# Spreading the decay rows of two mixers with a selector of 128 partitions instead of 64

## What is computed

```python
gc = jnp.cumsum(g, axis=-1)
decay = jnp.exp(jnp.where(incl, gc[..., :, None] - gc[..., None, :], -jnp.inf))
```

```python
acum = jnp.cumsum(da, axis=2)
seg = jnp.exp(jnp.where(incl, acum[:, :, :, None] - acum[:, :, None, :], -jnp.inf))
```

## Time and profile before

| what | before |
|---|---|
| median of 3 runs | 2264.95 us (2264.87 to 2265.81) |
| profiled execution, its own time | 2268.4 us |
| span of the profiled execution | 2266.6 us |
| TensorE busy | 2178.9 us, 96% of the span |
| TensorE weight loads busy | 1984.3 us, 88% |
| VectorE / ScalarE / GpSimd busy | 65% / 59% / 47% |
| mean granted TensorE clock | 0.981 |
| DMA | 151 GB/s read over the span |

### The profile page before, as it was taken

How to read it: one execution, slowest core, us unless ns; L and a number is a source line. 1 busy time by engine, 2 the same in 40 slices (tenths; PEclk the granted TensorE clock), 3 DMA queues, 4 the chain that set the end, 5 groups by cost and what they waited for, 6 DMA issues and landing times.

```text
span 2266.6 us, 46015 instructions
## 1 busy us (share of the span) xinstructions
PE 2178.9 (96%) x14384; PEld 1984.3 (88%) x14384; DVE 1476.7 (65%) x3206; ACT 1342.9 (59%) x2734; POOL 1069.7 (47%) x827
## 2 busy tenths in 40 slices
PE   7989699999999999999899988999999999999998
PEld 6979599999999988888797767999999999888886
DVE  5756319985666577777765452199756665777776
ACT  6754355577777544444475664555687785444444
POOL 6841378987666600000065337799976665000000
PEclk9989899999999999999999999999999999999999
DMA  5510254555444566666544224555554445666664
GB/s 167 167 58 1 66 176 149 168 165 157 139 139 139 171 190 192 194 194 194 177 133 136 65 66 150 166 159 168 167 155 139 139 139 167 194 193 192 191 194 147
DMA packets 93872, 343.66 MB, mean 152 GB/s; under 512 B 10688, under 2 KB 10752, under 8 KB 93152
## 3 DMA queue, kind: packets, MB, share of 16 engines
q1 hardware_dynamic: 92592, 338.21, 48.5%
q0 software_dynamic: 912, 4.07, 0.6%
q10 hardware_dynamic: 288, 0.34, 0.0%
HBM read 341.53 MB, written 1.05 MB: 151 GB/s over the span
## 4 chain that ended last, share of the span: by engine, by line
PE 82%; POOL 7%; issue 5%; DVE 3%; ACT 2%; DMA 1%; POOLq 0%; DVEq 0%; ACTq 0%
PE bank L359 80%; POOL w_lo L1738 7%; PE bank L524 0%; PE bank L379 0%; DMA small<-in_ssd_d 0%; ACT w_hi L1368 0%; ACT arena L1394 0%; DVE arena L874 0%; ACT arena L1368 0%; DVE arena L989 0%; DVE arena L1190 0%; DVE arena L1029 0%; DVE arena L925 0%; DMA ring<-in_norm_final 0%; ACT arena L1528 0%
## 5 line engine op out<-in xcount | busy, mean ns | idle before, releaser
L1738 POOL TENSOR_TENSOR w_lo<-ring,w_hi 128x512 fp32r<-128x512 f32 x744 | 993.5, 1350 | 685.6 <-ACT w_hi L1368 673.9
L1368 ACT ACTIVATE w_hi<-ring 128x512 fp32r<-128x512 f32 x1280 | 804.4, 630 | 544.5 <-PE bank L359 542.7
L359 PE MATMUL bank<-hT_hi,w_hi 128*128 128x256 f32 x2688 | 780.0, 290 | 9.1 <-POOL w_lo L1738 7.0
L359 PE MATMUL bank<-hT_lo,w_hi 128*128 128x256 f32 x2688 | 761.3, 283 | 0.0
L359 PE MATMUL bank<-hT_hi,w_lo 128*128 128x256 f32 x2688 | 761.2, 283 | 0.0
L359 PEld LDWEIGHTS bank<-hT_hi,w_hi 128*128 128x128 f32 x2688 | 516.2, 192 | 20.1 <-POOL w_lo L1738 19.6
L900 DVE TENSOR_TENSOR w_lo<-ring,w_hi 128x512 fp32r<-128x512 f32 x536 | 374.9, 699 | 220.9 <-ACT w_hi L1368 213.9
L359 PEld LDWEIGHTS bank<-hT_lo,w_hi 128*128 128x128 f32 x2688 | 516.5, 192 | 0.0
L359 PEld LDWEIGHTS bank<-hT_hi,w_lo 128*128 128x128 f32 x2688 | 515.8, 192 | 0.0
L359 PE MATMUL bank<-w_hi,p_ag_hi 128*128 128x512 f32 x1024 | 398.4, 389 | 0.0
L359 PE MATMUL bank<-w_lo,p_ag_hi 128*128 128x512 f32 x1024 | 398.4, 389 | 0.0
(11 more groups left out here) (241 smaller groups left out, 2256.8 us busy)
## 6 DMA issues: line engine op xcount, KB each, us to landing
ring<-in_peer_u SPq DMA_DIRECT2D x256, 512.0 KB, 3.5
ring<-in_peer_v SPq DMA_DIRECT2D x256, 512.0 KB, 3.7
ring<-in_peer_wq SPq DMA_DIRECT2D x32, 512.0 KB, 3.5
ring<-in_gdn_qkv SPq DMA_DIRECT2D x24, 512.0 KB, 3.6
ring<-in_ssd_xbc SPq DMA_DIRECT2D x24, 512.0 KB, 3.6
ring<-in_ssd_z SPq DMA_DIRECT2D x16, 512.0 KB, 3.5
ring<-in_ssd_out SPq DMA_DIRECT2D x16, 512.0 KB, 3.6
ring<-in_gdn_z SPq DMA_DIRECT2D x8, 512.0 KB, 3.5
```

The source lines that it names most:

```text
L359: return pe.matmul(o, w, r, start=first, stop=last)
L1368: return act.activation(o, i, ACT.Copy, scale=scale)
L1738: pool.tensor_tensor(w_part[1][:, s, :], ring[:, n % RING, hf * 512:(hf + 1) * 512], w_part[0][:, s, :].bitcast(F32), ALU.subtract).then_i ...
```

## The change

`pick` gets 128 partitions, of which the lower 64 are zero, and `s_row` is all 128 partitions of `p_ag[0]`. So the matmul with `pick` has weights of 128 x 128 instead of 64 x 128, in both mixers. The products of the lower 64 partitions are zero times what lies in `p_ag[0]` there. ScalarE makes one more copy in each mixer, from a zero block of the identity (partitions 64 to 127, columns 0 to 31), and the waits for `picks` count 3 and 6 instead of 2 and 4. The zeroing in GDN covers 128 partitions instead of 64. Nothing changes places.

```diff
-        pick = sb("pick", [2 * SH, SH], F32R)[:, :]
-        s_row = flat(p_ag[0][0:2 * SH, :, :], "s t")
+        pick = sb("pick", [P, SH], F32R)[:, :]
+        s_row = flat(p_ag[0][:, :, :], "s t")
...
-                mm(bank[:, :], pick[:, h:h + 1].to_broadcast([2 * SH, P]), s_row[:, :], True, False)
+                mm(bank[:, :], pick[:, h:h + 1].to_broadcast([P, P]), s_row[:, :], True, False)
...
-                pe.wait_ge(picks, 2)
+                pe.wait_ge(picks, 3)
...
-                pe.wait_ge(picks, 4)
+                pe.wait_ge(picks, 6)
...
-                        mm(o, pick[:, h:h + 1].to_broadcast([2 * SH, P]), s_row[:, st * P:(st + 3) * P], True, False)
+                        mm(o, pick[:, h:h + 1].to_broadcast([P, P]), s_row[:, st * P:(st + 3) * P], True, False)
...
-                        dve.tensor_scalar(p_ag[0][0:2 * SH, 1, :], flat(const[0:2 * SH, 0:2, :], "m i"), 0.0, None, ALU.mult)
+                        dve.tensor_scalar(p_ag[0][:, 1, :], flat(const[:, 0:2, :], "m i"), 0.0, None, ALU.mult)
...
                 copy(pick[SH:2 * SH, :], const[SH:2 * SH, C_EYE, SH:2 * SH]).then_inc(picks, 1)
+                copy(pick[2 * SH:P, :], const[2 * SH:P, C_EYE, 0:SH]).then_inc(picks, 1)
```

## The result

| what | before | after |
|---|---|---|
| median of 4 runs each | 2265.38 us (2264.87 to 2266.22) | 2239.09 us (2238.46 to 2239.70) |
| profiled execution, its own time | 2268.4 us | 2239.61 us |
| span of the profiled execution | 2266.6 us | 2237.8 us |
| TensorE busy | 2178.9 us | 2149.9 us |
| mean granted TensorE clock | 0.981 | 0.982 |

The ratio is 0.9879, with a 95% interval from 0.9863 to 0.9894: 26.3 us faster between the medians. The forecast was 2238.2 us in a range from 2232 to 2249, so time, range and sign are right. The steps behind the number are less right than the number, as the experiments show.

The account below looks back on a forecast made before the run. TensorE's distances between matmul starts were taken to bound all SSD heads and GDN until head 4. SSD 24.9 plus GDN 1.85 gave 26.75 us off 2268.4, then 3.45 down to the runs' median: 2238.2 us, range 2232 to 2249.

Parts of the forecast that it names:

- What bounds the kernel: TensorE is the chain through all 32 SSD heads, 127.14 us, and the first five GDN heads, 20.73 us.
- The cause: Weight loads of 64 partitions can't run ahead among those of 128; the form alone makes the loader wait, 15.1 us in SSD.
- The broadcast rival: Loads of a broadcast column can't run ahead either; 16.0 us won in SSD, some 1.4 in GDN: 2248 us; chance 0.08.
- no effect: The form is not the cause, every distance between matmuls stays, time 2265 us; chance 0.06.
- A matmul with `pick`, SSD, 25.3 us: SSD heads: distances between matmul starts fall from 1.71 to 0.92 us, 0.79 us a head, 25.3 us for 32.
- the three bursts: SSD: ScalarE's table loads, as at head 10, leave its exponentials just in time; cost 0, upper bound 0.3 us each.
- a sign that it is wrong: TensorE waiting for ScalarE's exponentials at heads 13, 21 and 29, or `pick` still having 0.3 us or more before it.
- The last head: SSD head 31: TensorE is 0.79 us earlier, ScalarE only 0.3 to 0.4, so 0.4 us is lost before the tail.
- GDN, 1.85 us: GDN: 0.39 us for each of four heads plus head 4's first two distances; VectorE is the chain from head 4.
- What is added, 0: One ScalarE copy per mixer, wider zeroing in GDN and higher `picks` count are covered; cost 0, bound 0.5 us in all.
- The clock: The profiled clock fell from 1.0 to 0.5 mid-SSD, costing 3.4 us; its going would give 2234.8, not counted, chance 0.28.
- The bounds: SSD `pick` matmuls: nothing if loads still wait, 0.87 us a head (27.8 in all) if columns stream at 2.4 GHz.

Follow-up runs that it names:

- the kernel that only fills: Changed kernel's added copies, wider zeroing and wait counts, but all `pick` matmuls read 64 partitions; 2266.52 us, ratio 1.0002 to the kernel before.

## Why the prediction was right, step by step

- **What bounds the kernel**: right. TensorE's distances in SSD set the time, and SSD alone gives the whole gain.
- **The cause**: right, and now shown from both sides: with half the changes of form half the gain arrives, and 96 partitions do as well as 128. "The broadcast rival" falls with the first timeline after; so does "no effect".
- **A matmul with `pick`, SSD, 25.3 us**: a head wins 0.78 us and not 0.79, and there are 31 distances between 32 heads. 31 x 0.79 = 24.5 would have been due, the distances without the clock give 22.65 (25.77 less 3.12). The missing 1.8 us: 0.7 behind heads 8, 16 and 24, most of it at the last two (0.28 each), where TensorE now waits for VectorE's copies (line 1160), which the forecast didn't look at; 0.7 at the three bursts; 0.3 from 0.78 in place of 0.79; and 0.2 at head 0.
- **"I cost the three bursts at 0, with 0.3 us each as the upper bound"**: they cost 0.22 each, heads 12 and 13 taking 3.09 us instead of 2.98. The bound was right, the value was too low. TensorE does wait for ScalarE's exponentials at heads 13, 21 and 29. The prediction had called that a sign that it is wrong, and on this one term it was.
- **The last head, 0.4 us lost**: more was lost. Of its 0.79 us the forecast left 0.39; what stands behind the `pick` of head 31, up to the output projection, got 0.16 us shorter. With that SSD gave 22.8 us, and 24.9 was forecast.
- **GDN, 1.85 us**: this step failed. Head 0 won nothing, and the step took VectorE for the last engine and named nothing that was late next. GpSimd was. About 0.95 us reach TensorE by the profiles, and the timed runs don't show even that.
- **What is added, 0**: right, 1.0002 in the kernel that only fills.
- **The clock**: "If the timed runs had it too and it goes, the time is 3.4 lower: 2234.8. I can't see that from one profile, and don't count it." It did go. By the profiles the timed runs did have it: it is in each profile of that form, three of three. It was worth 3.1 us. The profiled execution was 3.45 us above the median, and I took that for a hint that the others didn't have the fall. It was not one: the profile of the kernel that only fills has the fall too, at 2264.85 us, the lowest of its own ten runs. Its heads of SSD take 116.83 us against 116.82, and its first `pick` of SSD is at 1221.97 and not at 1225.24. So the difference between these two profiles lies ahead of the heads.
- **The bounds**: 0.87 us a head is 0.86 by its own terms (1.71 less 0.213 and 4 x 0.16), 27.4 us in all, and with it, 3.1 and 3.4 the low end of the range comes out near 2231 and not 2232. Nothing hangs on it.

So the number is better than its parts, and that is luck: 3.1 us of clock that I left out stand against 2.1 of SSD and 0.9 of GDN that I counted and that didn't come. 22.8 + 3.1 + 0.95 = 26.8 us is what the profiles account for, and the medians differ by 26.3.

## What to carry to other kernels

Where short matmuls alternate between weights of 64 partitions and weights of 96 or 128, pad the smaller ones with zero rows, or group them: each change cost 0.2 us here, four times for each of 32 heads. Count such a gain only on the engine that has no one beside it; where another is within a microsecond, name it, since what is won beyond that goes to it. Where the profile merges several matmuls into one row, look at them one by one before saying which distance holds the cost. And look for a fall of the clock in more than one profile of the same form before leaving it out of a sum.

## What the runs showed of the hardware

- A change between weights of 64 and of 128 partitions costs about 0.2 us: 0.10 in the distance in which it happens (0.33 against 0.23) and 0.10 in the next one (0.27 against 0.17). Where each distance is a change, it is 0.37 against 0.17 at 384 columns.
- A load of 64 partitions runs ahead of a streaming matmul of 64 (by 0.17 us), and one of 128 ahead of one of 128 (by 0.23). Across a change neither does.
- 96 partitions belong to the form of 128: 2.99 us a head, against 2.98 and 3.76.
- The clock fell from 1.00 to 0.50 with TensorE recorded as busy throughout, at one and the same head in each of three profiles, for 3.1 us of time, and two closer spreads ahead of that place kept it at 1.00. Why the like places at heads 8 and 24 never fell stays open.
- Behind the idle stretch after the heads of GDN the full clock came back 35.1 to 38.3 us after the first `pick` there, over twelve profiles. A gain of under a microsecond at such a place can't be read from one pair of profiles.
